# Two-block network (latent attention, gated recurrence, expert lookups) on one core: early identity and root table, latent norm's sums inside the sixth projection, its chain split in two

## The reference, cut to what matters

```python
def _rmsnorm(x, g):
    xf = x.astype(jnp.float32)
    y = xf * lax.rsqrt(jnp.mean(xf * xf, axis=-1, keepdims=True) + NORM_EPS)
    return (y * g.astype(jnp.float32)).astype(x.dtype)

def _mla(h, cos, sin, w_in, q_norm, w_q_up, kv_norm, w_kv_up, w_out):   # h is _rmsnorm(x, ln_mix[0])
    z = h @ w_in                                   # 384 + 256 + 64 columns
    c_q = z[..., :MLA_Q_LORA]
    c_kv = z[..., MLA_Q_LORA:MLA_Q_LORA + MLA_KV_LORA]
    k_rope = _rope(z[..., MLA_Q_LORA + MLA_KV_LORA:], cos, sin)
    q = (_rmsnorm(c_q, q_norm) @ w_q_up).reshape(B, S, MLA_HEADS, MLA_NOPE + MLA_ROPE)
    ...
    kv = (_rmsnorm(c_kv, kv_norm) @ w_kv_up).reshape(B, S, MLA_HEADS, MLA_NOPE + MLA_V)
    ...
```

## Time and profile before

| | us |
|---|---|
| three runs, median | 3083.33 |
| three runs, lowest and highest | 3080.94, 3085.20 |
| the profiled execution, its own time | 3083.25 |
| its span, first to last instruction | 3081.2 |
| PE busy in it | 3013.4 (98%) |
| DVE, ACT and POOL busy | 2354.5, 1202.7, 1317.2 |
| TensorE clock granted, mean share of full | 0.981 |

### The profile page before, as it was taken

The page is one execution under the profiler, slowest core; times in us unless marked ns, Lnnn a source line. Parts: engine busy times, 40 slices in busy tenths (PEclk is TensorE's granted clock), DMA queues, the critical chain, the costliest instruction groups (busy, mean ns, idle before and its releaser), DMA issues.

```text
span 3081.2 us, 43953 instructions
## 1 busy us (share of the span) xinstructions
PE 3013.4 (98%) x16132; PEld 2662.8 (86%) x16132; DVE 2354.5 (76%) x4427; ACT 1202.7 (39%) x1879; POOL 1317.2 (43%) x749
## 2 busy tenths in 40 slices
PE   7999999999999999999999999999999999999998
PEld 5658899999998888888788888999999997888887
DVE  5345899998987888888335647899888968888887
ACT  4433333444443333333434433334444434333333
POOL 3303465443434444443345433465444435443442
PEclk9899999999999999999998789999999999999999
DMA  3203266999999999998221003367999999999996
GB/s 137 74 14 103 95 200 243 340 376 356 376 365 383 361 361 356 351 357 325 94 96 62 1 28 110 115 206 279 358 359 370 366 367 378 367 351 347 365 352 254
DMA packets 345718, 800.83 MB, mean 260 GB/s; under 512 B 27937, under 2 KB 191777, under 8 KB 345249
## 3 DMA queue, kind: packets, MB, share of 16 engines
q1 hardware_dynamic: 271776, 529.55, 49.3%
q0 software_dynamic: 73728, 268.47, 23.0%
HBM read 695.15 MB, written 102.76 MB: 259 GB/s over the span
## 4 chain that ended last, share of the span: by engine, by line
PE 91%; DVE 3%; DMA 3%; issue 1%; ACT 1%; SPq 0%; POOL 0%; DVEq 0%; ACTq 0%
PE PS L1449 28%; PE PS L1451 27%; PE PS L1450 27%; PE PS L1617 3%; DMA arena<-acts_dram 1%; PE PS L1688 1%; PE PS L1594 1%; PE PS L1555 1%; DMA gates_dram<-arena 1%; PE PS L1572 1%; PE PS L1554 1%; PE PS L1730 0%; PE PS L1691 0%; PE PS L1562 0%; PE PS L1707 0%
## 5 line engine op out<-in xcount | busy, mean ns | idle before, releaser
L1449 PE MATMUL PS<-x_hi,w_hi 128*128 128x384 f32 (+1 forms) x2616 | 924.4, 353 | 15.2 <-issue 7.5
L611 ACT ACTIVATE w_hi<-w_raw 128x1024 fp32r<-128x1024 f32 x609 | 643.3, 1057 | 684.3 <-PE PS L1451 671.6
L1451 PE MATMUL PS<-x_hi,w_lo 128*128 128x384 f32 (+1 forms) x2616 | 907.9, 347 | 0.0
L1450 PE MATMUL PS<-x_lo,w_hi 128*128 128x384 f32 (+1 forms) x2616 | 906.7, 347 | 0.0
L550 POOL DMA_INDIRECT arena<-in_v_t,arena x256 | 445.8, 1741 | 600.1 <-DVE resid L1238 550.1
L1449 PE MATMUL PS<-w_hi,x_hi 128*128 128x512 f32 x1744 | 679.4, 390 | 5.5 <-DVE x_lo L1255 5.4
L1451 PE MATMUL PS<-w_hi,x_lo 128*128 128x512 f32 x1744 | 678.6, 389 | 0.0
L1450 PE MATMUL PS<-w_lo,x_hi 128*128 128x512 f32 x1744 | 678.5, 389 | 0.0
L539 POOL TENSOR_TENSOR w_lo<-w_raw,w_hi 128x1024 fp32r<-128x1024 f32 x169 | 419.1, 2484 | 572.8 <-ACT w_hi L611 572.7
L1215 DVE TENSOR_TENSOR w_lo<-w_raw,w_hi 128x1024 fp32r<-128x1024 f32 x440 | 537.3, 1221 | 109.1 <-ACT w_hi L611 104.5
L550 POOL DMA_INDIRECT arena<-in_u_rows,arena x256 | 381.1, 1489 | 487.1 <-DVE arena L1222 433.8
(11 more groups left out here) (183 smaller groups left out, 2421.4 us busy)
## 6 DMA issues: line engine op xcount, KB each, us to landing
w_raw<-in_u_t SPq DMA_DIRECT2D x256, 512.0 KB
w_raw<-in_v_t SPq DMA_DIRECT2D x256, 512.0 KB
acts_dram<-arena SPq DMA_DIRECT2D x256, 192.0 KB
gates_dram<-arena SPq DMA_DIRECT2D x24, 2048.0 KB
arena<-gates_dram SPq DMA_DIRECT2D x64, 768.0 KB
arena<-acts_dram SPq DMA_DIRECT2D x256, 192.0 KB
w_raw<-in_hg_t SPq DMA_DIRECT2D x40, 512.0 KB
w_raw<-in_pq_t SPq DMA_DIRECT2D x32, 512.0 KB
```

The source lines that it names most:

```text
L611: act.activation(w_hi[:, slot, :], w_raw[:, slot, :], ACT.Copy).then_inc(hi_ready, 1)
L1449: pe.matmul(ps, wh, xh, start=start, stop=False)
L1450: pe.matmul(ps, wh, xl, start=False, stop=False)
L1451: return pe.matmul(ps, wl, xh, start=False, stop=stop)
```

## The change

Start of the program. ACT itself issues the transfer of the 128 identity columns, as its first instruction, with a semaphore of its own, `ident_in`, on which PE's transposes wait. SP loads the other 386 columns of the constants after z1, and PE waits for them ahead of z0. The gains come before z0. DVE writes a one into a spare column of `stat`; ACT takes a root of it ahead of the norm. ACT rounds z0 and z1 before the `x_hi` casts, z2 and z3 after them.

Latent norm. PE issues the five products with ones after three of the eight blocks of z5, then the other five blocks, then z6 block by block, with a count `latent_room` after each of the first five. ACT takes the two roots ahead of `next_high(5)`. Each latent cast on ACT waits for its `latent_room`, and `next_high(6)` comes after the casts. DVE goes through the query part as a whole (reciprocal, three scaled latents, three `x_lo`), then through the part of keys and values, then multiplies z5 by the cosine. The banks of `zss` are freed by a semaphore of their own.

```diff
--- before.py
+++ after.py
@@ -185,11 +185,11 @@
             b.add((name, n), frees, last_tile if n == 7 else None, banks)
 
     norm(0)
-    for m in range(7):
-        if m == 6:
-            b.add(("zss", 0), "dve")
-            b.add(("zss", 1), "dve")
+    for m in range(6):
         b.add(("z", m), "dve" if m >= 5 else "act", BASE["z"] + m)
+    for n in range(2):
+        b.add(("zss", n), "sum")
+    b.add(("z", 6), "dve", BASE["z"] + 6)
     for m in range(16):
         end = 3 * m + 2
         b.add(("q_up", m), "act" if m < 8 else "dve", BASE["q_up"] + end // 8 if end % 8 == 7 else None)
@@ -454,9 +454,9 @@
 
             for t in range(TT):
                 sp.dma_start(resid[:, t, :], x[t * P:(t + 1) * P, :]).then_inc(x_in[t], 16)
-            sp.dma_start(const[:, :], consts).then_inc(sem("const_in"), 16)
             sp.dma_start(gain[:, :], gains).then_inc(sem("gain_in"), 16)
             load_range("z", 2)
+            sp.dma_start(const[:, P:C_COLS], consts[:, P:C_COLS]).then_inc(sem("const_in"), 16)
             sp.dma_start(posi, pos.partition_broadcast(P)).then_inc(sem("pos_in"), 16)
             load_range("z", 23, 2)
             sp.dma_start(mask_bits[:, :], masks).then_inc(sem("mask_in"), 16)
@@ -636,7 +636,7 @@
 
                 rstd_of_resid(k)
                 if k == 0:
-                    for n in range(RING):
+                    for n in range(2):
                         high(n, n, 0)
                     act.wait_ge(sem("gain_in"), 16)
                 else:
@@ -648,7 +648,12 @@
                     act.activation(x_hi[:, c, :], PSb(("xT", k, c)), ACT.Copy,
                                    scale=gain[:, g:g + 1]).then_inc(sem("x_high"), 1)
 
+            act.dma_start(ident, consts[:, 0:P]).then_inc(sem("ident_in"), 16)
+            act.wait_ge(sem("one_made"), 1)
+            act.activation(stat[:, 12:13], stat[:, 12:13], ACT.Sqrt)
             norm(0)
+            for n in range(2, RING):
+                high(n, n, 0)
 
             for n in range(2):
                 act.wait_ge(sem("angle"), n + 1)
@@ -657,16 +662,18 @@
                 if m < 5:
                     ready(act, ("z", m))
                     free(act.activation(zT[:, m, :], PSb(("z", m)), ACT.Copy), ("z", m))
-                next_high(BASE["z"] + m)
                 if m == 5:
                     for n in range(2):
                         act.wait_ge(sem("latent_mean"), n + 1)
                         act.activation(tmp[:, n, :], tmp[:, n, :], ACT.Sqrt)\
                            .then_inc(sem("latent_root"), 1)
-            ready(act, ("z", 6))
+                if m < 6:
+                    next_high(BASE["z"] + m)
             for m in range(5):
+                act.wait_ge(sem("latent_room"), m + 1)
                 act.wait_ge(sem("latent"), m + 1)
                 act.activation(x_hi[:, m, :], zT[:, m, :], ACT.Copy).then_inc(sem("latent_high"), 1)
+            next_high(BASE["z"] + 6)
             for m in range(16):
                 if m < 8:
                     ready(act, ("q_up", m))
@@ -976,6 +983,7 @@
                 was_freed(dve, (name, 2 * t + 1))
                 dve.sem_inc(sem("resid_done"), 1)
 
+            dve.memset(stat[:, 12:13], 1.0).then_inc(sem("one_made"), 1)
             norm(0)
 
 
@@ -1013,27 +1021,26 @@
                 was_freed(dve, ("z", m))
                 dve.tensor_tensor(qn[:, m, :], zT[:, m, :], zT[:, m, :], ALU.mult)\
                    .then_inc(sem("latent_sq"), 1)
-            ready(dve, ("z", 5))
-            free(dve.tensor_tensor(kr, PSb(("z", 5)), cosT, ALU.mult), ("z", 5))
             for n, width in enumerate((Q_LORA, KV_LORA)):
                 ready(dve, ("zss", n))
                 free(dve.tensor_scalar(tmp[:, n, :], PSb(("zss", n)), 1.0 / width, EPS, ALU.mult, ALU.add),
                      ("zss", n))
                 was_freed(dve, ("zss", n))
                 dve.sem_inc(sem("latent_mean"), 1)
-            for n in range(2):
+            for n, ms in enumerate((range(QC), range(QC, QC + VC))):
                 dve.wait_ge(sem("latent_root"), n + 1)
                 chain(dve.reciprocal(tmp[:, n, :], tmp[:, n, :]))
-            for m in range(5):
-                g = G_AT["q"] + m if m < QC else G_AT["kv"] + m - QC
-                dve.scalar_tensor_tensor(zT[:, m, :], zT[:, m, :], gain[:, g:g + 1],
-                                         tmp[:, 0 if m < QC else 1, :], ALU.mult, ALU.mult)\
-                   .then_inc(sem("latent"), 1)
+                for m in ms:
+                    g = G_AT["q"] + m if m < QC else G_AT["kv"] + m - QC
+                    dve.scalar_tensor_tensor(zT[:, m, :], zT[:, m, :], gain[:, g:g + 1], tmp[:, n, :],
+                                             ALU.mult, ALU.mult).then_inc(sem("latent"), 1)
+                for m in ms:
+                    dve.wait_ge(sem("latent_high"), m + 1)
+                    dve.tensor_tensor(x_lo[:, m, :], zT[:, m, :], f32(x_hi[:, m, :]), ALU.subtract)\
+                       .then_inc(sem("latent_low"), 1)
+            ready(dve, ("z", 5))
+            free(dve.tensor_tensor(kr, PSb(("z", 5)), cosT, ALU.mult), ("z", 5))
             ready(dve, ("z", 6))
-            for m in range(5):
-                dve.wait_ge(sem("latent_high"), m + 1)
-                dve.tensor_tensor(x_lo[:, m, :], zT[:, m, :], f32(x_hi[:, m, :]), ALU.subtract)\
-                   .then_inc(sem("latent_low"), 1)
             was_freed(dve, ("z", 5))
             rotate(kr, None, PSb(("z", 6)), ("z", 6))
             for j in range(4):
@@ -1450,11 +1457,11 @@
                 pe.matmul(ps, wh, xl, start=False, stop=False)
                 return pe.matmul(ps, wl, xh, start=False, stop=stop)
 
-            def across(ps, slot, normed=None):
+            def across(ps, slot, normed=None, first=0, last=KC):
 
 
                 cols = ps.shape[-1]
-                for kc in range(KC):
+                for kc in range(first, last):
                     if normed is not None:
                         was_freed(pe, ("xT", normed, kc))
                     w = slice(kc * P, (kc + 1) * P)
@@ -1508,17 +1515,28 @@
                         if i == TT - 1:
                             end(mm, ("xT", k, c))
 
+            pe.wait_ge(sem("ident_in"), 16)
+            norm(0)
             pe.wait_ge(sem("const_in"), 16)
-            norm(0)
-            for k in range(6):
+            for k in range(5):
                 projection("z", k, 0)
+            wait_low(pe, BASE["z"] + 5)
+            begin(("z", 5))
+            across(PSb(("z", 5)), (BASE["z"] + 5) % RING, None, 0, 3)
             for n, ms in enumerate((range(0, QC), range(QC, QC + VC))):
                 begin(("zss", n))
                 for m in ms:
                     pe.wait_ge(sem("latent_sq"), m + 1)
                     mm = pe.matmul(PSb(("zss", n)), ones, qn[:, m, :], start=m == ms[0], stop=m == ms[-1])
                 end(mm, ("zss", n))
-            projection("z", 6)
+            end(across(PSb(("z", 5)), (BASE["z"] + 5) % RING, None, 3), ("z", 5))
+            wait_low(pe, BASE["z"] + 6)
+            begin(("z", 6))
+            for kc in range(KC):
+                mm = across(PSb(("z", 6)), (BASE["z"] + 6) % RING, None, kc, kc + 1)
+                if kc < QC + VC:
+                    mm.then_inc(sem("latent_room"), 1)
+            end(mm, ("z", 6))
 
             def blocks_of(name, count, kcs, x_at):
 
```

## The result

| | kernel before | changed kernel |
|---|---|---|
| median of the first comparison, us | 3081.90 (6 runs) | 3066.07 (6 runs, 3063.22 to 3070.95) |
| ratio to before, 95% interval | | 0.9947 (0.9936 to 0.9959) |
| ratio in a second comparison (e14) | | 0.9943 (0.9929 to 0.9956) |
| profiled execution | 3083.25 | 3063.22 |
| first projection matmul on PE, us | 18.63 | 15.58 |

The changed kernel is faster by 0.5%. The ratio stands for 16 us, 12.6 to 19.7. The prediction had 13.9 us. The start and the latent norm went nearly as foretold; 12.6 us are won by the first score. The other 7 lie where the prediction saw nothing, in the attention.

What follows compares the result with a forecast made beforehand. PE was taken to bound the kernel, held up by late z2/z3 loads and DVE's latent-norm chain. Gains of 3.3 + 7.5 + 3.1 = 13.9 us off 3083.25 gave 3069.4, range 3066 to 3074.5.

Steps and rivals of the forecast that it cites:

- The start: Start of the program: x_hi casts and first projection come earlier, gaining 3.0 to 3.9 us, 3.3 taken.
- the latent norm: Ahead of q_up: PE's whole 7.47 us idle goes, and the low clock after it, another 3.1 us.
- the three waits of the earlier trace: PE's waits in the first 100 us: 9.6 for constants, 3.4 for the first x_lo, 7.5 put down to issue.
- issue: Listed cause of PE's 7.5 us wait ahead of q_up, read as DVE's chain of reciprocals, scaled latents and x_lo.
- rival (1): Clock still at 0.50 when the projections start, costing at most 3.1 us; time 3072.5, chance 0.10.
- The slack of 1.1 us: Latent norm: DVE's query x_lo were to be ready 1.1 us before PE wants them for q_up.
- rival (2): Latent norm's slack missing: q_up waits 1 to 3 us, too short for low clock; 3070.5 to 3072.5, chance 0.07.
- (3): Start does not move: identity and x hinder each other, x lands 3 us later; 3072.7, chance 0.05.
- (4): Start slower: ACT's identity transfer lands very late, delaying PE's transposes; 3088 if at 27 us, chance 0.02.
- (5): Fixing one stall uncovers another at the same place (bank of z5, tile 10), giving back over 7; 3078, chance 0.04.
- Later stages are counted from PE's own progress and shift whole: Everything after the latent norm, attention included, moves earlier by the summed 13.9 us, with no further gain or loss.
- the range: Foretold span of the changed kernel's time, 3066 to 3074.5 us, said to leave out under 2 in 10.

Runs made afterwards that it cites:

- e14: The changed kernel measured again, unchanged; median 3064.68 us, ratio 0.9943 to the kernel before.
- e9: Changed kernel plus one unused 512-column product with ones on PE ahead of k_up; median 3066.45 us, ratio 0.9954.
- e11: Changed kernel plus three unused products with ones on PE ahead of k_up; median 3070.32 us, ratio 0.9960.
- e13: Kernel before plus eight unused products with ones in PE's idle ahead of q_up; median 3076.32 us, ratio 0.9985.
- e12: Changed kernel with z0/z1 copies and z4/z5 rounding ahead of the sines, tile 9's rounding behind the query casts, on ACT; 3064.08 us, 0.9945.
- e7: Changed kernel with the sums put back between z5 and z6, chain still split; median 3067.19 us, ratio 0.9957.
- e8: Changed kernel with DVE's latent chain in one again, sums still inside z5; median 3068.81 us, ratio 0.9964.
- e10: Changed kernel plus two unused products with ones on PE ahead of k_up; median 3065.00 us, ratio 0.9952.
- e2: Kernel before with only the latent norm half of the change; median 3072.31 us, ratio 0.9962.
- e4: Kernel before with only the start's new loads and early root table, z2 and z3 still rounded ahead of the casts; 3083.91 us, 1.0004.
- e1: Kernel before with only the start half of the change, latent norm as before; median 3071.30 us, ratio 0.9966.
- e3: Kernel before with only the rounding of z2 and z3 moved behind the x_hi casts; median 3076.53 us, ratio 0.9983.
- e5: Kernel before plus four unused dense products with ones among the first attention scores; median 3082.34 us, ratio 1.0008.
- e6: Changed kernel plus four unused dense products with ones among the first attention scores; median 3064.00 us, ratio 0.9949.

## Why the prediction was right or wrong

**What bound the kernel** was read rightly: the three waits of the earlier trace rows are what the change removed, and "issue" was DVE's chain.

**The start, 3.3 taken, 3.0 to 3.9 as bounds: right in the profile, 3.05**; e9 and e11, where the transposes' faster pace came earlier, reach the other bound (4.0, 4.1), and the changed kernel's first `x_hi` at 13.86 lies between 13.1 and 14.0. The step that failed here is one that isn't in the sum. The prediction looked for a low clock in the changed kernel, as rival (1), and found none in the kernel before, because its one profiled execution had none. Four of the five profiles with a wait of PE of 2.7 to 4.0 us have it. The change also removes that, 1.7 to 2.7 us in such executions. Rival (1) itself is refuted: in all eleven kernels with the short wait the projections began at 1.00. The Trainium skill (TensorE: Matmul & The Clock Gate, Part 4: PE-mode transpose) says that the full clock does not come on with transposes. The traces disagree: in all sixteen profiles the transposes' pace rose amid them, from 421 to 272 ns each.

**The latent norm, 7.5 + 3.1 foretold, 7.17 + 2.9 measured** (e13 for the second). Against it stands 0.4 us at z4, where PE waited for `w_lo`. The slack of 1.1 us, rival (2)'s subject, was not there: the three scaled latents took 4.22 instead of 2.77. e12 shows why: POOL's subtraction of tile 9 lay beside them. The prediction took DVE's durations from rows without asking what POOL did then. The error was worth 0.3 us, as the chain still nearly met z6's end. Rival (2)'s price also counted on a wait of 1 to 3 us being too short for the low clock. e7 and e8 refute that: waits of 1.96 and 2.87 had 3.4 us of it behind them. Rivals (3), (4) and (5) did not come. x landed 0.5 us later, not 3, but the prediction had allowed 0.2 at most.

**"Later stages are counted from PE's own progress and shift whole"** is the step that failed in the sum. They do shift whole in work. But the attention's own length is 77.8 us or some 85, by whether the granted clock falls at its start: 84.9 in the profile of before, 77.8 in that of the changed kernel. The stretch at 0.50 from 129.6 to 146.7 stood in the trace of before, outside the first 100 us that the prediction read. Had both executions met the fall, the difference would have been 12.6 to 13, and 3083.25 - 12.6 = 3070.7, inside the range. Without the fall it is 3063.2, outside. The spread of 4.3 us over three runs, on which the range was built, was too small: before's runs in all comparisons go from 3072.8 to 3088.9, and the changed kernel's from 3061.5 to 3071.

**The medians.** They differ by 15.8 and, in the second comparison, by 16.9, where the sum said 13.9. The groups of runs account for it. Within the group of higher clock the change gives 3077.6 - 3065.4 = 12.2 us, as much as the 12.6 by which the scores are earlier; the rest comes from the group of lower clock, some 6 us slower, that the change leaves nearly empty. That the forecast of 13.9 is near to 16 is thus partly luck: it had no term for this.

**What stays open.** Why the change thins out that group. The early fall is in one of the six profiles of the changed kernel without products in the attention (e11; the changed kernel, e9, e10, e12 and e14 have none), and in four of eight profiles of before or with a part of the change (before, e2, e4, e8 against e1, e3, e7, e13). e1 keeps the whole idle ahead of q_up, and yet only two of its seven runs are at 0.982 or 0.983. So the idle alone isn't what decides it, and e9 and e10 say that a later start of the attention doesn't bring the fall back, while e11's runs leave that open for 2.6 us. The late fall of the attention, in eight of the sixteen profiles, has no cause shown either.

## What to carry to other kernels

When a row of waits names a value, follow the chain back to the instruction in front of it in its engine's list: here a cast waited for the rounding of two weight tiles it didn't need. Moving that behind the cast gave 1.7 us; making the data earlier gave nothing alone. A reduction whose sums can be taken inside a longer product, and a chain cut so that only the part needed first comes first, each hid more than half of an idle of 7.5 us. Price an idle of PE with the clock after it, short ones too. Look over the whole trace for stretches below full clock before a single execution's difference is taken as the change's, and sort the runs by their mean clock before their medians are compared.

## What the runs showed of the hardware

- DVE and POOL. The cast of the positions took 0.42 us at 23.00 in the kernel before, with POOL idle, and 2.46 in the changed one, where POOL was making the `w_lo` of z2 and z3 (19.61 to 24.56):

```profile
19.85 2.46 DVE L993 CAST arena<-arena 128x512 f32<-128x512 int32 x1
22.34 2.50 DVE L995 TENSOR_SCALAR arena<-arena,const 128x512 f32<-128x512 f32 x1
```

  Each is about as long as one POOL instruction (4.95 for two). The Trainium skill, SBUF — State Buffer, section "SBUF: two separate sides", says that the two share a port pair that some of DVE's instructions need, and that whichever engine starts first holds it for its whole instruction while the other waits. The trace agrees. It put the second sine off by 4 us (33.26; 29.3 is an estimate, before's 32.4 less the 3.05 of the start) and z4 by 0.4.
- The clock can fall over PE's wait of 2.7 to 4.0 us between 32 transposes and the first projection, in four of five profiles, and did not with 0.8 to 1.1 us, in eleven. It fell after idles of 1.96 us (e7) and 2.87 us (e8) between dense products, and not after 0.30 or 0.61.
- It fell early in the attention while PE counted as busy nearly throughout (22.63 of 23.00 us in the kernel before). With four dense products there (e5, e6) it did not fall there. Late in the attention it fell in eight of sixteen profiles, with such products or without.
- Behind 1400 us every one of the sixteen profiles has another 88 to 97 us at 0.50, in ten or eleven pieces; the change does not touch them.
- PE's 32 transposes go from 421 to 272 ns each amid their own run, at 11.5 to 15.5 us, where the trace's first record of the clock begins.
- The transfer of the identity, issued by ACT at 0.75 beside SP's of x, cost the first tile of x 0.5 us, more than its share of the bytes (64 KB of 2 MB): ACT's first square starts at 4.00 to 4.12 in the five profiles without it and at 4.54 to 4.67 in the eleven with it.
